# Loads of the cached values of sample batches 4 to 7 issued from ScalarE's queue instead of SyncE's, in a streaming encoder step

## The chip, the cores and the metric

The kernel runs on one core of one Trainium2 chip. The metric is the device time of one execution in microseconds (us). Before the change its median is 1579.01 us over 3 runs (1578.56 to 1579.61).

## What is computed

Two layers (`DEPTH` = 2) of a hybrid encoder run over 512 prompt tokens and 8 sample batches of 16 new tokens each. A layer has a combined input projection, three head groups side by side (retention, forgetting attention, a short convolution), an output projection and a gated feed-forward block. The part around the change is the forgetting attention of the sample batches: each batch's 16 new queries look at 512 cached keys and values and at their own 16 new ones.

```
def _fox_sample(q, k, v, logf, ck, cv, clogf):
    k_all = jnp.concatenate([ck.astype(k.dtype), k], axis=1)
    v_all = jnp.concatenate([cv.astype(v.dtype), v], axis=1)
    c_t = jnp.transpose(jnp.cumsum(lf_all, axis=1), (0, 2, 1))
    sc = jnp.einsum('bqhd,bkhd->bhqk', q, k_all, preferred_element_type=jnp.float32) * scale
    sc = sc + cq[..., None] - c_t[:, :, None, :]
    sc = jnp.where(mask, sc, -jnp.inf)
    p = jax.nn.softmax(sc, axis=-1)
    return jnp.einsum('bhqk,bkhd->bqhd', p.astype(v_all.dtype), v_all)
```

For each batch the cached keys are 512 x 512 float32 (1 MiB), and so are the cached values. The forget bias of a batch (`c_t` above, 8 heads x 512) is spread over 128 partitions by a third load of 256 KiB.

## The kernel before, in words

The program is written by hand for five engines, which meet through semaphores. Large matrix products run on TensorE (PE) as three products of rounded high and low parts, all of them recorded at line 2218; turns of tiles are at line 2280. The weights come in slabs of 512 KiB through `raw`, a buffer of three slots; ScalarE (ACT) rounds a slab into `whi` (`upto`, line 1145), VectorE (DVE) forms the rest `wlo` (line 1521).

Sample attention handles the batches n = 0 to 7 in a fixed pipeline:

- PE: `scores(n)` (line 2533) multiplies the queries of batch n with its cached keys; `turned(n)` turns the probabilities of batch n-1; `values(n)` multiplies them with the cached values of batch n-1. The order is `scores(1)`, then for n = 1 to 7 `turned(n)`, `scores(n + 1)`, `values(n)`; between the last steps the first products of the output projection are put (`out_slab`).
- DVE: `maxima(n)` (line 1954) adds the bias to the scores and takes the maximum; it waits for the bias load of the batch.
- ACT: `exps(n)` (line 1364) takes the exponential, and line 1241 copies the turned probabilities from the PSUM bank to `pTs`. After the copies of n = 5, 6 and 7 ACT rounds a weight slab.
- SyncE (SP) issues all loads, in the order in which its program has them, and where it waits for a semaphore everything behind that stands still.

The cached keys have five buffers and the cached values four, so a load waits until an earlier batch has used its buffer:

```
        kcache = (kb, kx, kbo, ky, kT)
        vcache = (vb[:, 0], vx[:, :, :], vb[:, 1], vr[:, :, :])
K_HOME = (0, 1, 2, 3, 4, 0, 2, 4)
V_HOME = (0, 1, 2, 3, 0, 2, 3, 0)
```

In what follows K4 to K7 are the key loads of batches 4 to 7 (`load_k`, line 749, into `kT`, `kb`, `kbo`, `kT`), V4 to V7 the value loads (`load_v`, line 753, into `vb`, `vb`, `vr`, `vb`) and P4 to P7 the bias loads (`load_pb`, line 850, into `pb`). `("ss", n)` is the bank of `scores(n)`, `("so", n)` the bank of the values product of batch n, and `smax` counts finished `maxima`. SP's order before is K4, K5, P4, V4, P5, K6, P6, V5, P7, K7, V6, V7, and then the weight slabs 31 to 33 (line 718), each of which waits until its slot is free.

Of the kernel before, what the change touches and what calls it, by code (L numbers as in the profile page):

```python
# [37 lines left out]
P = 128  # L38
D = 1024
KT = D // P  # L40
SEQ, NB, NS, PAST = 512, 8, 16, 512
# [211 lines left out]
V_HOME = (0, 1, 2, 3, 0, 2, 3, 0)  # L253
# [114 lines left out]
def build(nc, a):  # L368
    with ExitStack() as ctx:
        sems = {}  # L370

        def sem(name):
            sems[name] = ctx.enter_context(nc.semaphore(name))
            return sems[name]

        bank = [ctx.enter_context(nc.psum_tensor(f"bank{i}", [P, 512], F32)) for i in range(8)]
        B = Banks([sem(f"full{i}") for i in range(8)], [sem(f"free{i}") for i in range(8)])
# [32 lines left out]
        def K(name):  # L410
# [21 lines left out]
        fbias = own("fbias", [P, FH])  # L432
        ftap = own("ftap", [P, 2, 3])
        (fqg, fkg, gng, t2f, qbd, ncp, _, pb1, pb2) = region(
            [("fqg", [P, FW], F32), ("fkg", [P, FW], F32), ("gng", [P, RW], F32)],
            [("t2f", [P, 4, HALF], F32)],
            [("qbd", [P, 2, P], F32), ("ncp", [P, SEQ], F32)],
            [("by_qbd", [P, 2, P], F32), ("pb1", [P, PAST], F32), ("pb2", [P, PAST], F32)])
        (gains, os_, ncc, _, pb0) = region(
            [("gains", [P, D], F32)],  # L440
            [("os", [P, 4, P], F32), ("ncc", [P, PAST], F32)],
# [6 lines left out]
             ("t2h", [P, 4, HALF], F32R), ("t2l", [P, 4, HALF], F32R), ("s1", [P, 512], F32), ("s2", [P, 512], F32)])  # L448
        (gs, t4h) = region([("gs", [P, TT, RW], F32)], [("t4h", [P, 4, HALF], F32R)])
        (rT, kw, rv, decp, decq, st, _, decs, s0, _, lfxh, lfxl, kb, kT, vb, _, pTf, _, ycv, gpad, gu, _, lrows, t4l, s3, s4, _, _, _, h21, h22,  # L450
         _, _, _, xlo, xhi, _, pb3) = region(
            [("rT", [P, 4, NTOK], F32), ("kw", [P, TT, RW], F32), ("rv", [P, TT, RW], F32),
# [33 lines left out]
        vcache = (vb[:, 0], vx[:, :, :], vb[:, 1], vr[:, :, :])  # L486
# [57 lines left out]
        v_in = [sem(f"v_in{i}") for i in range(4)]  # L544
# [158 lines left out]
        def _(sp):  # L703
# [44 lines left out]
            def load_k(l, b):  # L748
                sp.dma_start(kcache[K_HOME[b]][:, :, :], kview[bass.ds(l * NB + b, 1)].rearrange("o p g n -> p (o g) n"))\
                    .then_inc(k_in[K_HOME[b]], 16)  # L750

            def load_v(l, b):
                sp.dma_start(vcache[V_HOME[b]], vview[bass.ds(l * NB + b, 1)].rearrange("o p k n -> p (o k) n"))\
                    .then_inc(v_in[V_HOME[b]], 16)
# [15 lines left out]
            for l in range(DEPTH):  # L770
# [113 lines left out]
                def next_pb(b):  # L884
                    sp.wait_ge(smax, l * NB + b - 3)
                    load_pb(b)
# [5 lines left out]
                B.wait_full(sp, ("ss", 0), l)  # L892
                load_k(l, 5)
                next_pb(4)
                B.wait_full(sp, ("so", 0), l)
                load_v(l, 4)
                next_pb(5)
                B.wait_full(sp, ("ss", 2), l)
                load_k(l, 6)
                next_pb(6)  # L900
                B.wait_full(sp, ("so", 2), l)
                load_v(l, 5)
                next_pb(7)
                B.wait_full(sp, ("ss", 4), l)
                load_k(l, 7)
                B.wait_full(sp, ("so", 3), l)
                load_v(l, 6)
                B.wait_full(sp, ("so", 4), l)
                load_v(l, 7)

                for n in range(31, 34):
                    load(n, l, slab_src(n, l))
# [224 lines left out]
        def _(act):  # L1137
# [9 lines left out]
            def upto(n, l):  # L1147

                while split_to[0] <= n:
                    if split_to[0] >= SLOTS or l == 0:  # L1150
                        wait_used(act, split_to[0] - SLOTS, l)
                    elif split_to[0] == 0:
                        B.wait_full(act, ("u", "loop", "a4"), l - 1, PAIRS - 2)
                    else:
                        B.wait_full(act, ("d", "end", split_to[0] - 1, TT - 1), l - 1)
                    split(split_to[0], l)
                    split_to[0] += 1
# [76 lines left out]
            for l in range(DEPTH):  # L1234
                split_to[0] = 0

                def evac(key, out, l, it=None, view=None):

                    B.wait_full(act, key, l, it)
                    src = bank[B.bank(key)][:, :] if view is None else view(bank[B.bank(key)])  # L1240
                    act.activation(out, src, ACT.Copy).then_inc(B.free[B.bank(key)], 1)
# [117 lines left out]
                def exps(n):  # L1359

                    act.wait_ge(smax, l * NB + n + 1)
                    o = SB + 8 * (n % 3)
                    for c0, n_, acc in ((0, PAST, 3), (PAST + NS * n, NS, 4)):
                        act.activation(ps[:, n % 2, c0:c0 + n_], ps[:, n % 2, c0:c0 + n_], ACT.Exp, scale=-1.0,
                                       bias=col(o + 2), accum_out=col(o + acc)).then_inc(sexp, 1)
# [2 lines left out]
                    exps(n)  # L1368
                for n in range(1, NB + 1):
                    evac(("pt", n - 1), pTs[:, (n - 1) % 2, 0:512], l)  # L1370
                    if n in (5, 6, 7):
                        B.wait_full(act, ("so", 3), l)
                        upto(WO + n - 5, l)
                    if n + 1 < NB:
                        exps(n + 1)
# [1395 lines left out]
```

## Time and profile before

| | |
|---|---|
| median of 3 runs | 1579.01 us (1578.56 to 1579.61) |
| the profiled execution: its own time | 1580.97 us |
| the profiled execution: span of the core | 1579.2 us |
| mean granted TensorE clock | 0.993 of full speed |
| PE busy | 1544.2 us, 98% of the span |
| DVE busy | 1053.8 us, 67% |
| ACT busy | 667.0 us, 42% |
| GpSimd busy | 401.5 us, 25% |
| moved by DMA | 168.02 MB, mean 106 GB/s |

The span runs from the first to the last instruction. PE is busy nearly all the time, so a microsecond in which it stands still is a microsecond of the total. The loads and stores are all but a few issued by SP and run on one hardware queue of the 16 DMA engines (queue q1 of the profile: 166.95 of the 168.02 MB). Engine names with a q behind them (SPq, ACTq) are the issuing of transfers, which is not counted as busy. "To landing" is the time from the issue of a transfer until its semaphore has its full count.

### The profile page before, as it was taken

To read this page: it belongs to the slowest core of one execution; us is meant where nothing else is said; L and a number is where in the kernel's file an instruction comes from. 1 tells how busy PE (TensorE), PEld (TensorE's weight loads), DVE (VectorE), ACT (ScalarE), POOL (GpSimd) and SP (SyncE) were. 2 spreads that over 40 slices of the span, in tenths; PEclk is the share of its full clock that TensorE was granted. 3 is DMA by queue.
4 is the path that set the end of the run, shared out by engine and by line. 5 is a ranking of instruction groups with operands and counts; after the bars stand their busy time and mean duration, and the time that the engine had idled before them with its cause. 6 is when DMAs were issued, how large, how long until landed. Compare 5 with 4: busy or idle time off the path is not lost.

```text
span 1579.2 us, 28383 instructions
## 1 busy us (share of the span) xinstructions
PE 1544.2 (98%) x9892; PEld 1347.8 (85%) x9892; DVE 1053.8 (67%) x1815; ACT 667.0 (42%) x1246; POOL 401.5 (25%) x505
## 2 busy tenths in 40 slices
PE   8999999799999999999999999988999999999998
PEld 6878896589999999999888789856899999999997
DVE  4445447339988888888654552662599888788885
ACT  4223327226444444444433233462365444444442
POOL 1113100004433333333112140000144333333330
PEclk9999999899999999999999999998999999999999
DMA  7213446622322222222242225574223222222222
GB/s 231 81 56 85 143 159 253 200 81 67 94 80 81 90 85 89 83 90 68 79 108 67 72 82 183 181 243 149 81 72 114 82 80 80 80 80 80 82 77 73
DMA packets 119005, 168.02 MB, mean 106 GB/s; under 512 B 28217, under 2 KB 80349, under 8 KB 114798
## 3 DMA queue, kind: packets, MB, share of 16 engines
q1 hardware_dynamic: 118784, 166.95, 33.9%
q8 instruction: 47, 0.77, 0.2%
q14 instruction: 28, 0.23, 0.0%
q10 hardware_dynamic: 146, 0.07, 0.0%
HBM read 157.11 MB, written 9.89 MB: 106 GB/s over the span
## 4 chain that ended last, share of the span: by engine, by line
PE 90%; DVE 4%; DMA 3%; ACT 1%; issue 1%; DVEq 0%; POOL 0%; POOLq 0%; SPq 0%; ACTq 0%
PE bank L2218 87%; PE bank L2280 3%; DMA kT<-in_cache_fox_k 2%; DVE pf L1881 0%; DMA raw<-in_w_gate 0%; DVE pf L1894 0%; DVE gulo L1545 0%; DMA raw<-in_w_in 0%; DVE x L2005 0%; DVE xn L1573 0%; DVE wlo L1535 0%; DVE wlo L1541 0%; POOLq L1112 0%; DVE wlo L1521 0%; POOL s L1110 0%
## 5 line engine op out<-in xcount | busy, mean ns | idle before, releaser
L2218 PE MATMUL bank<-whi,hhi 128*128 128x512 f32 x560 | 225.2, 402 | 0.9 <-DVE hlo L1545 0.6
L2218 PE MATMUL bank<-whi,hlo 128*128 128x512 f32 x560 | 219.4, 392 | 0.0
L2218 PE MATMUL bank<-wlo,hhi 128*128 128x512 f32 x560 | 218.9, 391 | 0.0
L2218 PE MATMUL bank<-hhi,whi 128*128 128x320 f32 x640 | 198.7, 310 | 0.8 <-DVE hlo L1545 0.8
L2218 PE MATMUL bank<-hhi,wlo 128*128 128x320 f32 x640 | 197.8, 309 | 0.0
L2218 PE MATMUL bank<-hlo,whi 128*128 128x320 f32 x640 | 197.6, 309 | 0.0
L2218 PE MATMUL bank<-whi,guhi 128*128 128x512 f32 x440 | 171.7, 390 | 0.4 <-DVE gulo L1545 0.4
L2218 PE MATMUL bank<-wlo,guhi 128*128 128x512 f32 x440 | 171.3, 389 | 0.0
L2218 PE MATMUL bank<-whi,gulo 128*128 128x512 f32 x440 | 171.2, 389 | 0.0
L1521 DVE TENSOR_TENSOR wlo<-raw,whi 128x1024 fp32r<-128x1024 f32 x80 | 100.1, 1251 | 106.5 <-ACT whi L1145 105.1
L2005 DVE TENSOR_TENSOR x<-x,bank 128x512 f32<-128x512 f32 x220 | 142.9, 682 | 29.0 <-PE bank L2218 27.5
L1145 ACT ACTIVATE whi<-raw 128x1024 fp32r<-128x1024 f32 x80 | 84.5, 1058 | 109.2 <-PE bank L2218 100.5
L2218 PEld LDWEIGHTS bank<-whi,hhi 128*128 128x128 f32 x560 | 105.7, 189 | 25.4 <-issue 3.0
L2218 PEld LDWEIGHTS bank<-whi,hlo 128*128 128x128 f32 x560 | 105.5, 188 | 22.9
L2218 PEld LDWEIGHTS bank<-wlo,hhi 128*128 128x128 f32 x560 | 105.9, 189 | 20.0
L2218 PEld LDWEIGHTS bank<-hhi,whi 128*128 128x128 f32 x640 | 120.2, 188 | 2.7 <-issue 1.9
L2218 PEld LDWEIGHTS bank<-hlo,whi 128*128 128x128 f32 x640 | 120.2, 188 | 0.8
L2218 PEld LDWEIGHTS bank<-hhi,wlo 128*128 128x128 f32 x640 | 120.1, 188 | 0.0
L1110 POOL TENSOR_TENSOR s<-raw 128x512 f32<-128x512 f32 x60 | 91.4, 1523 | 84.3 <-DMA raw<-in_w_gate 84.3
L1110 POOL TENSOR_TENSOR s<-raw,gains 128x512 f32<-128x512 f32 x20 | 27.3, 1363 | 311.0 <-DMA raw<-in_w_up 311.0
L990 POOL TENSOR_SCALAR small<-small 128x1 f32<-128x1 f32 (+2 forms) x42 | 12.3, 292 | 338.6 <-ACT xn L1218 214.8
L2218 PEld LDWEIGHTS bank<-whi,gulo 128*128 128x128 f32 x440 | 82.6, 188 | 17.4
(303 smaller groups left out, 3581.4 us busy)
## 6 DMA issues: line engine op xcount, KB each, us to landing
raw<-in_w_in SPq DMA_DIRECT2D x52, 512.0 KB, 3.7
raw<-in_w_gate SPq DMA_DIRECT2D x44, 512.0 KB, 3.8
raw<-in_w_down SPq DMA_DIRECT2D x44, 512.0 KB, 3.5
raw<-in_w_up SPq DMA_DIRECT2D x24, 512.0 KB, 3.7
vb<-in_cache_fox_v SPq DMA_DIRECT2D x10, 1024.0 KB, 9.6
gains<-in_w_up SPq DMA_DIRECT2D x20, 512.0 KB, 3.7
raw<-in_w_out SPq DMA_DIRECT2D x16, 512.0 KB, 3.8
bcr<-scr_p SPq DMA_DIRECT2D x8, 512.0 KB, 5.1
```

What stands on the lines that cost most here:

```text
L990: pool.tensor_scalar(col(var, n), col(ss, n), scale, EPS, ALU.mult, ALU.add)
L1110: pool.tensor_tensor(by_k(out[:, :]), x_, y_, op).then_inc(s_sum, 1)
L1145: act.activation(whi[:, slot(n), 0:width(n)], raw[:, slot(n), 0:width(n)], ACT.Copy).then_inc(hi_split, 1)
L1521: dve.tensor_tensor(wlo[:, s_, 0:w_], raw[:, s_, 0:w_], whi[:, s_, 0:w_].bitcast(F32), ALU.subtract).then_inc(lo_split, 1)
L2005: dve.tensor_tensor(x[:, t, 512 * c:512 * c + 512], x[:, t, 512 * c:512 * c + 512], bank[B.bank(key)][:, :], ALU.add).then_inc(B.free[B.ba ...
L2218: return pe.matmul(out, lhsT=lhsT, rhs=rhs, start=start, stop=stop, skip_group_check=True)
L2280: ins = pe.transpose(dst, src, ident[0:src.shape[0], 0:src.shape[0]])
```

## The change

SP no longer issues V4 to V7. Its waits for the banks `("so", 0)`, `("so", 2)`, `("so", 3)` and `("so", 4)` go with them. ACT issues the four loads instead, behind its copies of n = 2, 4, 5 and 6, with the same waits, the same addresses and the same buffers. The queue is then ACT's own. Nothing else is changed; V0 to V3 stay with SP.

```
                 load_k(l, 5)
                 next_pb(4)
-                B.wait_full(sp, ("so", 0), l)
-                load_v(l, 4)
                 next_pb(5)
                 B.wait_full(sp, ("ss", 2), l)
                 load_k(l, 6)
                 next_pb(6)
-                B.wait_full(sp, ("so", 2), l)
-                load_v(l, 5)
                 next_pb(7)
                 B.wait_full(sp, ("ss", 4), l)
                 load_k(l, 7)
-                B.wait_full(sp, ("so", 3), l)
-                load_v(l, 6)
-                B.wait_full(sp, ("so", 4), l)
-                load_v(l, 7)
...
                 for n in range(1, NB + 1):
                     evac(("pt", n - 1), pTs[:, (n - 1) % 2, 0:512], l)
+                    if n in (2, 4, 5, 6):
+                        b, before = {2: (4, 0), 4: (5, 2), 5: (6, 3), 6: (7, 4)}[n]
+                        B.wait_full(act, ("so", before), l)
+                        act.dma_start(vcache[V_HOME[b]], a["cache_fox_v"].rearrange("l b (p k) h d -> (l b) p k (h d)", p=P)
+                                      [bass.ds(l * NB + b, 1)].rearrange("o p k n -> p (o k) n")).then_inc(v_in[V_HOME[b]], 16)
                     if n in (5, 6, 7):
                         B.wait_full(act, ("so", 3), l)
                         upto(WO + n - 5, l)
```

On SP, from K5 to the weight slabs, the order before is the following (`full2` is the semaphore of a bank filled by `scores`, `full5` of the bank filled by `values`; buffer numbers stand behind `pb`):

```order
L749 DMA kb<-in_cache_fox_k 128x2048 [waits full2]
L850 DMA pb_87<-scr_c 128x1x512 [waits smax]
L753 DMA vb<-in_cache_fox_v 128x2048 [waits full5]
L850 DMA pb_81<-scr_c 128x1x512 [waits smax]
L749 DMA kbo<-in_cache_fox_k 128x2048 [waits full2]
L850 DMA pb_82<-scr_c 128x1x512 [waits smax]
L753 DMA vb<-in_cache_fox_v 128x2048 [waits full5]
L850 DMA pb_140<-scr_c 128x1x512 [waits smax]
L749 DMA kT<-in_cache_fox_k 128x2048 [waits full2]
L753 DMA vr<-in_cache_fox_v 128x2048 [waits full5]
L753 DMA vb<-in_cache_fox_v 128x2048 [waits full5]
L718 DMA raw<-in_w_out 128x2x512 [waits lo_split] x3
```

With the change it is this:

```order
L749 DMA kb<-in_cache_fox_k 128x2048 [waits full2]
L850 DMA pb_87<-scr_c 128x1x512 [waits smax]
L850 DMA pb_81<-scr_c 128x1x512 [waits smax]
L749 DMA kbo<-in_cache_fox_k 128x2048 [waits full2]
L850 DMA pb_82<-scr_c 128x1x512 [waits smax]
L850 DMA pb_140<-scr_c 128x1x512 [waits smax]
L749 DMA kT<-in_cache_fox_k 128x2048 [waits full2]
L718 DMA raw<-in_w_out 128x2x512 [waits lo_split] x3
```

The two V loads that stood ahead of K7 and the two that stood behind it are gone; P5 follows P4, P7 follows P6, and K7 follows P7.

On ACT, around the steps n = 4 to 6 of the sample batches, the changed kernel has this order (its lines stand 8 above those of the kernel before, so 1233 is the copy to `pTs`, 1356 `exps`, 1137 the rounding of a slab):

```order
L1233 ACTIVATE pTs<-bank 128x512 [waits full6]
L1366 DMA vb<-in_cache_fox_v 128x2048 [waits full5]
L1356 ACTIVATE ps,small<-ps,small 128x512 [waits smax]
L1356 ACTIVATE ps,small<-ps,small 128x16
L1233 ACTIVATE pTs<-bank 128x512 [waits full1]
L1366 DMA vr<-in_cache_fox_v 128x2048 [waits full5]
L1137 ACTIVATE whi<-raw 128x1024 [waits raw_in1,full0,full5]
L1356 ACTIVATE ps,small<-ps,small 128x512 [waits smax]
L1356 ACTIVATE ps,small<-ps,small 128x16
L1233 ACTIVATE pTs<-bank 128x512 [waits full6]
L1366 DMA vb<-in_cache_fox_v 128x2048 [waits full5]
```

V5, V6 and V7 now stand between a copy and the next exponentials, V6 also ahead of the rounding of a slab; V4 stands in the same way behind the copy of n = 2.

## Rows read from the trace of the kernel before

**Rows 1.** Page, part 4: the chain that ended last, by line

```profile
PE bank L2218 87%; PE bank L2280 3%; DMA kT<-in_cache_fox_k 2%; DVE pf L1881 0%; DMA raw<-in_w_gate 0%; DVE pf L1894 0%; DVE gulo L1545 0%; DMA raw<-in_w_in 0%; DVE x L2005 0%; DVE xn L1573 0%; DVE wlo L1535 0%; DVE wlo L1541 0%; POOLq L1112 0%; DVE wlo L1521 0%; POOL s L1110 0%
```

**Rows 2.** The chain in order of time: start us, us, what

```profile
278.84 15.61 DMA kT<-in_cache_fox_k
...
1060.74 14.98 DMA kT<-in_cache_fox_k
```

**Rows 3.** Timeline of PE, layer 0: start us, us, line, form, count [idle before <-releaser]

```profile
285.33 1.93 PE L2218 MATMUL bank<-kbo,qbd 128*32 128x512 f32 x8 [0.42 <-DMA kbo<-in_cache_fox_k]
...
294.49 1.93 PE L2218 MATMUL bank<-kT,qbd 128*32 128x512 f32 x8 [4.26 <-DMA kT<-in_cache_fox_k]
296.20 1.93 PE L2218 MATMUL bank<-vb,pTs 128*32 128x128 f32 x32
```

**Rows 4.** Timeline of PE, layer 1

```profile
1075.76 1.94 PE L2218 MATMUL bank<-kT,qbd 128*32 128x512 f32 x8 [4.18 <-DMA kT<-in_cache_fox_k]
```

**Rows 5.** Timeline of SP's issues, layer 0: P5, K6, P6, V5, P7, K7, V6, V7, slab

```profile
271.50 0.60 SPq L850 DMA_DIRECT2D pb<-scr_c  x1
272.14 0.46 SPq L749 DMA_DIRECT2D kbo<-in_cache_fox_k  x1
272.64 0.60 SPq L850 DMA_DIRECT2D pb<-scr_c  x1
277.83 0.32 SPq L753 DMA_DIRECT2D vb<-in_cache_fox_v  x1
278.19 0.60 SPq L850 DMA_DIRECT2D pb<-scr_c  x1
278.84 0.46 SPq L749 DMA_DIRECT2D kT<-in_cache_fox_k  x1
281.52 0.33 SPq L753 DMA_DIRECT2D vr<-in_cache_fox_v  x1
289.18 0.33 SPq L753 DMA_DIRECT2D vb<-in_cache_fox_v  x1
290.77 0.38 SPq L718 DMA_DIRECT2D raw<-in_w_out  x1
```

**Rows 6.** By tile, one issue each: time to landing of K6, V5, K7, V6, V7

```profile
DMA to landing us min/median/max: 13.1/13.1/13.1
...
DMA to landing us min/median/max: 12.5/12.5/12.5
...
DMA to landing us min/median/max: 15.6/15.6/15.6
...
DMA to landing us min/median/max: 15.4/15.4/15.4
...
DMA to landing us min/median/max: 10.2/10.2/10.2
```

**Rows 7.** Stretches: us, busy time of each engine, PEclk, DMA share, GB/s

```profile
267.50:294.50 27.00, 18.88 (x324) 11.00 (x325) 13.15 (x69) 11.77 (x34) 1.91 (x9) 0.89 0.99 325
...
278.00:280.50 2.50, 2.16 (x35) 0.91 (x37) 1.09 (x6) 1.43 (x5) 0.18 (x1) 1.00 1.00 231
...
292.00:295.50 3.50, 1.01 (x8) 0.35 (x12) 0.00 (x0) 0.00 (x0) 0.00 (x0) 0.51 0.95 374
```

**Rows 8.** By tile `vr`, whole run (V3 and V6 of both layers): time to landing

```profile
DMA to landing us min/median/max: 4.7/9.9/15.4
```

**Rows 9.** Timeline of ACT, layer 0, copies and exponentials of n = 4 to 6

```profile
278.86 0.57 ACT L1241 ACTIVATE pTs<-bank 128x512 f32<-128x512 f32 x1
...
284.18 0.58 ACT L1241 ACTIVATE pTs<-bank 128x512 f32<-128x512 f32 x1
...
288.52 0.72 ACT L1364 ACTIVATE ps<-ps,small 128x512 f32<-128x512 f32 x1 [2.82 <-DVE small L1958]
...
289.73 0.60 ACT L1241 ACTIVATE pTs<-bank 128x512 f32<-128x512 f32 x1
```

**Rows 10.** Timeline of DVE, layer 0, `maxima` of batch 6

```profile
287.44 0.69 DVE L1954 CUSTOM_DVE_ANT_0 ps<-bank,pb 128x512 f32<-128x512 f32 x1 [2.01 <-DMA pb<-scr_c]
```

More of the change, by code:

```diff
@@ L894, in _ @@
                 next_pb(4)
-                B.wait_full(sp, ("so", 0), l)
-                load_v(l, 4)
                 next_pb(5)
@@ L900, in _ @@
                 next_pb(6)
-                B.wait_full(sp, ("so", 2), l)
-                load_v(l, 5)
                 next_pb(7)
@@ L905, in _ @@
                 load_k(l, 7)
[L906 to L909, printed above, removed]
                 for n in range(31, 34):
@@ L1370, in _ @@
                     evac(("pt", n - 1), pTs[:, (n - 1) % 2, 0:512], l)
+                    if n in (2, 4, 5, 6):
+                        b, before = {2: (4, 0), 4: (5, 2), 5: (6, 3), 6: (7, 4)}[n]
+                        B.wait_full(act, ("so", before), l)
+                        act.dma_start(vcache[V_HOME[b]], a["cache_fox_v"].rearrange("l b (p k) h d -> (l b) p k (h d)", p=P)
+                                      [bass.ds(l * NB + b, 1)].rearrange("o p k n -> p (o k) n")).then_inc(v_in[V_HOME[b]], 16)
                     if n in (5, 6, 7):
```

## The prediction

> **What bounds the kernel now.** I read the chain of waits first. It is PE from end to end, and the only transfer in it with a share worth naming is the load of `kT` with 2% [rows 1]. In order of time that is one piece per layer, 15.61 and 14.98 us from issue to landing [rows 2]; it is K7, the keys of batch 7. So the place is the sample attention, and every microsecond by which K7 lands earlier or later moves all that comes after it.
>
> The timeline of PE says what K7 costs: PE stands still for 4.26 us before `scores(7)` in layer 0 and 4.18 us in layer 1 [rows 3, 4]. PE reached that point at 294.49 - 4.26 = 290.2 us. It also waited 0.42 us for K6 [rows 3], and DVE waited 2.01 us for P6 [rows 10]. All three waits are for loads of one family.
>
> The issues of SP [rows 5] and the times to landing [rows 6] then give the queue. K6 lands at 272.1 + 13.1 = 285.2, V5 at 277.8 + 12.5 = 290.3, K7 at 278.8 + 15.6 = 294.4, V6 at 281.5 + 15.4 = 296.9, V7 at 289.2 + 10.2 = 299.4. The loads land in the order of issue, and 1 MiB that took 4.7 us in a nearly empty queue [rows 8] takes 10 to 16 here. The stretches say why: from 267.5 to 294.5 the DMA engines are busy for a share of 0.99 [rows 7]. **The bound of this piece is the work in the DMA engines, not the moment at which SP issues.** Two prices follow from the differences of the landings. V6 and V7 cost 2.5 us each with nothing between them, P7 and K7 together 294.4 - 290.3 = 4.1. And of 4.7 us in an empty queue some 2.2 are not transfer (4.7 - 2.5), so a load begins to move about 2 us after its issue.
>
> **The change part by part.** A move on SP: K7 waits for `scores(4)` and stands behind V5 and P7. Without the V loads it is issued some 2 us sooner, since V5 at 277.83 and P7 are what stands right ahead of it [rows 5]. Worth: nothing, because K7 lies 15.6 us in a queue that is never empty; an earlier place in line only helps past what is ahead of it. The same goes for P5 and P6, K5 and K6. Their order among themselves stays.
>
> Four issues on ACT. An issue by SP takes 0.32 us [rows 5], and I take 0.4. The waits added before them are for values products that PE does before the turns whose result ACT has just copied, so they are met on arrival. Behind the issue stand the exponentials, and ACT stood still 2.82 us before those of batch 6 [rows 9], which hides the 0.4 us also where a slab is rounded between. Worth: nothing. If that cover went, it would be 4 x 0.4 = 1.6 us per layer.
>
> The new order in the DMA engines is what counts. Before, everything is served in one line: V4 and V5 ahead of K7, V6 and V7 behind it. Now the V loads have a line of their own. V4 and V5 are still served before K7 ends: V5 is issued behind the copy at 278.86 + 0.57 [rows 9], begins to move near 282 and has until 294. They cost K7 what they cost before. V6 is new ahead of K7. It is issued behind the copy that ends at 284.18 + 0.58 = 284.8 [rows 9], and moves from about 287. At 287 the SP line still holds part of P6, P7 and K7, and K7's landing is 7.4 us of work away, with V6 9.9. V6 needs 2.5 us of these 9.9, so it is done before K7 whenever ACT's line gets more than a quarter of the service. Cost: **+2.5 us per layer**.
>
> V7 is issued behind the copy at 289.73 + 0.60 [rows 9]. That copy stands behind the exponentials of batch 6, which need P6, and P6 is now late itself: in the one line it did not wait for V5, now V5 (2.5 us) and a part of V6 go between, some 3.5 us. So V7 is issued near 290.3 + 3.5 = 293.8 and moves from about 296, when K7 (due at 296.9) lacks about 1 us. It takes as much again from K7 if the two take turns. Cost: **+1.0 us per layer**.
>
> PE arrives at `scores(7)` later too, as K6 shares with V5 from 282 and lands up to 285.2 - 282 = 3.2 us, with turns half of it, later. PE is there near 292, still well before 297.9, so this adds nothing; the wait for K7 grows from 4.3 to near 6. Behind `scores(7)` the values of batches 5 and 6 find V5 and V6 landed, and V7 is wanted only after the first slabs of the output projection. The slab at 290.77 waits for its slot and not for SP [rows 5]. TensorE's granted clock is already at its lower level, 0.51 of full speed, which is 1.2 of 2.4 GHz, while PE waits for K7 [rows 7]; I add nothing for a longer wait.
>
> Sum: 2.5 + 1.0 = 3.5 us per layer, 7.0 us for two. The profiled execution has 1580.97 us (span 1579.2) and would come to 1588.0; it stands 1.96 above the median, so against the median the forecast is 1579.0 + 7.0 = **1586.0 us**.
>
> No row of this trace shows two lines that share the DMA engines. The bounds for that are these. At worst V6 and V7 both go whole before K7: 5.0 us per layer. At best SP's line is served first: K7 lands at least 2.5 us sooner and PE has it at about 291.9, but the next product needs V5, which then lands when K7 did, at 294.4, and that product began at 296.20 [rows 3]: -1.8 us per layer. I take a value near the upper end, because a quarter of the service for ACT's line is enough for the larger term.
>
> The Trainium skill, DMA: Bandwidth & Descriptors, section Queues, rings and completion order, has it that each DMA engine takes turns between the queues that have work, a packet at a time. By that rule V6 is served ahead of K7 and the sum is the +2.5 to +5.0 us per layer; without it -1.8 would be as good a guess. Its section Issuing engines are not separate DMA queues says that issuing from several engines saves only issue time, which speaks against the change. No run here shows either yet.
>
> **The rivals.** *The two lines together move more.* The rate while bias loads are under way falls to 231 GB/s, and without them it is 374; the mean over the piece is 325 [rows 7]. If packets of the other line filled these holes, the 27 us would become 27 x 325 / 374 = 23.5, that is 3.5 us less, just what the order costs: 1579 us, no change. Against it: the DMA share is 1.00 in the hole as well, so the engines were not idle in it. Half of that effect gives 1582.5.
>
> *SP's line is served first* (the other side). ACT's loads only get what is left. K7 then comes at once when its buffer and P7 allow, the wait of 4.26 us shrinks to what V5 needs, and the piece gains 1.8 us per layer: 1579.0 - 3.6 = 1575.4. It decides from the point where ACT's line gets under a quarter of the service after 287 us. For it: SP's loads are issued some 2 us earlier and stand in line in time. Against it: nothing in the rows favours a queue.
>
> *Nothing moves*, because K7 is not held up by what is ahead of it but by its own late issue. Then 2 us sooner would be 2 us gained per layer, 1575. Against it stand the landings in the order of issue.
>
> **How the numbers follow.** About 0.2%, 3.2 us, is what a measurement of this kernel tells from no change. The main case (V6, and V7 in part or whole, ahead of K7; 1584 to 1589) has 0.60, all slower. More throughput has 0.23: 0.17 of it within 0.2%, 0.03 just slower, 0.03 beyond it to faster. SP first or the late issue have 0.14: 0.11 faster, 0.03 within. The last 0.03 go to small mixed outcomes within 0.2%. That makes faster 0.14, within 0.23, slower 0.63. The range takes in the upper bound (1579 + 10 = 1589, and 1 us for a longer spell at the low clock) and the case of full throughput with some spread, 1577: 1577 to 1590.
>
> **What would show it.** In the changed profile queue q10 carries 8 MiB more. V6 lands before K7, K7 lands near 298 in layer 0 (294.4 before), PE waits near 6 us before `kT`, and DVE waits longer for P6 than 2.01 us. The forecast is wrong if V6 lands behind K7, if the rate of the piece is well over 325 GB/s, or if PE's wait for `kT` is shorter than 4.26 us.

## The result and the profile after

The changed kernel has a median of 1583.00 us over 9 runs (1578.09 to 1585.53), the kernel before 1579.01 us over 9 runs (1576.82 to 1580.57). The ratio is 1.0022, with a 95% interval from 1.0013 to 1.0031. By this ratio the change is 3.5 us slower (2.1 to 4.9); 7.0 us were forecast. The sign is right, the size is half. The profiled execution took 1582.30 us, its span is 1580.4 us.

The page of the changed kernel shows the eight loads on ACT's own queue, 8.46 MB on q10 in place of 0.07. The chain by line is as before [rows 1], with the load of `kT` at 2%.

```profile
span 1580.4 us, 28383 instructions
...
q1 hardware_dynamic: 117632, 158.56, 32.4%
q10 hardware_dynamic: 1298, 8.46, 1.5%
...
PE bank L2215 86%; PE bank L2277 3%; DMA kT<-in_cache_fox_k 2%; DVE pf L1878 0%; DMA raw<-in_w_gate 0%; DVE pf L1891 0%; DVE gulo L1542 0%; DVE x L2002 0%; DVE xn L1570 0%; DVE wlo L1532 0%; DVE wlo L1538 0%; ACT xn L1210 0%; DMA x<-in_x_prompt 0%; POOLq L1104 0%; DVE wlo L1518 0%
```

The issues of K4 and K7 by SP, and those of V5, V6 and V7 by ACT, in layer 0 of the changed kernel. SP issues K4 here at 264.83, 0.98 us earlier than before, by what happened long ahead of this place. So in what follows I count from the issue of K4.

```profile
264.83 0.33 SPq L749 DMA_DIRECT2D kT<-in_cache_fox_k  x1
...
275.65 0.33 SPq L749 DMA_DIRECT2D kT<-in_cache_fox_k  x1
```

```profile
277.41 0.33 ACTq L1366 DMA_DIRECT2D vb<-in_cache_fox_v  x1
...
281.52 0.33 ACTq L1366 DMA_DIRECT2D vr<-in_cache_fox_v  x1
...
291.61 0.72 ACT L1356 ACTIVATE ps<-ps,small 128x512 f32<-128x512 f32 x1 [8.29 <-DVE small L1955]
291.62 0.34 ACTq L1366 DMA_DIRECT2D vb<-in_cache_fox_v  x1
```

K7 is issued 10.8 us behind K4 (13.0 before, where K4 went out at 265.81), as SP no longer waits for values products. It lands 18.5 us after its issue, where it took 15.6 [rows 6]. V6 goes out at 281.52 and lands after 9.1 us, at 290.6, ahead of K7 (294.2); it landed behind it before. The times to landing, by tile, of K7, V6 and V7 of layer 0:

```profile
DMA to landing us min/median/max: 18.5/18.5/18.5
...
DMA to landing us min/median/max: 9.1/9.1/9.1
...
DMA to landing us min/median/max: 5.3/5.3/5.3
```

V7 is issued only at 291.62, in the same moment as the exponentials of batch 6, which had waited 8.29 us. What held them up is in the timelines of DVE and PE:

```profile
290.53 0.69 DVE L1951 CUSTOM_DVE_ANT_0 ps<-bank,pb 128x512 f32<-128x512 f32 x1 [7.48 <-DMA pb<-scr_c]
...
1072.93 0.69 DVE L1951 CUSTOM_DVE_ANT_0 ps<-bank,pb 128x512 f32<-128x512 f32 x1 [8.03 <-DMA pb<-scr_c]
```

```profile
284.06 1.94 PE L2215 MATMUL bank<-kbo,qbd 128*32 128x512 f32 x8 [1.52 <-DMA kbo<-in_cache_fox_k]
...
292.41 0.45 PE L2277 MATMUL bank<-const,ps 128*128 128x128 f32 x1 [4.04 <-issue]
...
294.24 1.94 PE L2215 MATMUL bank<-kT,qbd 128*32 128x512 f32 x8 [0.93 <-DMA kT<-in_cache_fox_k]
...
1077.03 1.94 PE L2215 MATMUL bank<-kT,qbd 128*32 128x512 f32 x8 [1.31 <-DMA kT<-in_cache_fox_k]
```

DVE waits 7.48 us for P6, against 2.01 [rows 10]. In DVE's program the scaling of batch 4's result stands behind `maxima(6)`, and PE's turn of that result, which stands ahead of `scores(7)`, waits for it. So the stop shows up on PE as 4.04 us at line 2277, and the wait at `kT` is short, 0.93 and 1.31 us, against 4.26 and 4.18 [rows 3, 4]. Reading only the wait that had been named before, one would call the change a gain. Counted from K4's issue, `scores(7)` begins at 29.4 and 30.3 us in the two layers, and began at 28.7 and 28.4: 0.7 and 1.9 us later.

Two stretches of layer 0 show a thing I had not read before (the last two columns are the DMA share and GB/s):

```profile
278.00:280.50 2.50, 2.38 (x53) 1.36 (x56) 1.41 (x8) 0.85 (x4) 0.46 (x2) 1.00 1.04 433
...
288.00:292.00 4.00, 0.38 (x4) 0.14 (x2) 1.23 (x8) 0.39 (x1) 0.00 (x0) 0.84 0.51 202
```

From 288 to 292, while P6 and K7 are still missing, the DMA engines are busy for a share of 0.51 only, and move 202 GB/s; from 278 to 280.5 it was 433. The share is a mean over 16 engines. I read it as half of them having nothing to do and the rest being late; e4 puts this to the test.

### The profile page after: what moved, and what is told of

The parts are those of the page before. It is cut to its first block, busy times and chain, and to the rows that moved or that the text cites. A ratio compares the mean times of both kernels' runs of the same rounds, so it can differ in the third digit from the quotient of the medians.

```text
span 1580.4 us, 28383 instructions
## 1 busy us (share of the span) xinstructions
PE 1544.4 (98%) x9892; PEld 1347.4 (85%) x9892; DVE 1053.5 (67%) x1815; ACT 666.3 (42%) x1246; POOL 401.4 (25%) x505
## 3 DMA queue, kind: packets, MB, share of 16 engines
q10 hardware_dynamic: 1298, 8.46, 1.5%
## 4 chain that ended last, share of the span: by engine, by line
PE 90%; DVE 4%; DMA 3%; ACT 1%; issue 1%; POOL 0%; DVEq 0%; POOLq 0%; SPq 0%; ACTq 0%
PE bank L2215 86%; PE bank L2277 3%; DMA kT<-in_cache_fox_k 2%; DVE pf L1878 0%; DMA raw<-in_w_gate 0%; DVE pf L1891 0%; DVE gulo L1542 0%; DVE x L2002 0%; DVE xn L1570 0%; DVE wlo L1532 0%; DVE wlo L1538 0%; ACT xn L1210 0%; DMA x<-in_x_prompt 0%; POOLq L1104 0%; DVE wlo L1518 0%
## 5 line engine op out<-in xcount | busy, mean ns | idle before, releaser
L2002 DVE TENSOR_TENSOR x<-x,bank 128x512 f32<-128x512 f32 x220 | 142.8, 681 | 29.2 <-PE bank L2215 28.5
```

The costliest lines, as they stand in the source:

```text
L2002: dve.tensor_tensor(x[:, t, 512 * c:512 * c + 512], x[:, t, 512 * c:512 * c + 512], bank[B.bank(key)][:, :], ALU.add).then_inc(B.free[B.ba ...
```

## The experiments

"K7 at" is the start of `scores(7)` in layer 0 and layer 1, counted from K4's issue, from the one profiled execution of each kernel. Each kernel was timed against the kernel before on the same chip (medians of before: 1579.75, 1580.05 and 1579.88 us in the three sets).

| run | edit | median us | ratio (95%) | K7 at |
|---|---|---|---|---|
| before | | 1579.01 | | 28.7, 28.4 |
| the change | V4 to V7 on ACT | 1583.00 | 1.0022 (1.0013 to 1.0031) | 29.4, 30.3 |
| e1 | V4, V5 on ACT | 1579.91 | 1.0002 (0.9993 to 1.0011) | 28.1, 28.8 |
| e2 | V6, V7 on ACT | 1589.04 | 1.0054 (1.0040 to 1.0067) | 33.3, 33.6 |
| e3 | the change, V6 and V7 one step later | 1577.28 | 0.9984 (0.9975 to 0.9993) | 29.1, 27.4 |
| e4 | before, bias source of 16 rows | 1572.49 | 0.9950 (0.9937 to 0.9964) | 24.7, 25.2 |
| e5 | the change, bias source of 16 rows | 1574.90 | 0.9965 (0.9951 to 0.9978) | 23.6, 28.5 |
| e6 | before, V5 issued behind K7 | 1577.05 | 0.9983 (0.9974 to 0.9992) | 26.3, 26.7 |
| e7 | e1 with e4 | 1571.59 | 0.9942 (0.9929 to 0.9956) | 23.4, 25.0 |
| e8 | e6 with e4 | 1568.73 | 0.9926 (0.9912 to 0.9939) | 23.7, 23.8 |
| e9 | before, V6 and V7 held until K7 has landed | 1578.02 | 0.9989 (0.9980 to 0.9998) | 27.5, 27.7 |
| e10 | before, V7 held until K7 has landed | 1578.82 | 0.9998 (0.9989 to 1.0007) | 28.9, 28.0 |

In layer 0 of six of these profiles (e3, e4, e5, e7, e8, e10) PE also stops inside a values product for 1.8 to 3.8 us, with no releaser that the profile names; in layer 1 only e8 has such a stop (2.0 us). In before, the change, e1, e6 and e9 there is none over 0.6 us. So in layer 0 of those six "K7 at" can hide a wait for K7 or be late by itself, and I give K7's landing where it matters.

**e1 and e2: which half of the change costs.** In e1 only V4 and V5 are left on ACT, in e2 only V6 and V7.

```
e1 (against the change)
                 load_k(l, 7)
+                B.wait_full(sp, ("so", 3), l)
+                load_v(l, 6)
+                B.wait_full(sp, ("so", 4), l)
+                load_v(l, 7)
-                    if n in (2, 4, 5, 6):
+                    if n in (2, 4):
e2 (against the change)
                 next_pb(4)
+                B.wait_full(sp, ("so", 0), l)
+                load_v(l, 4)
...
                 next_pb(6)
+                B.wait_full(sp, ("so", 2), l)
+                load_v(l, 5)
-                    if n in (2, 4, 5, 6):
+                    if n in (5, 6):
```

> Half of the change is taken back: V4 and V5 stay on ACT, V6 and V7 are issued by SP behind K7 as before. Theory (order): the loss comes from V6 being served ahead of P6 and K7, so it goes: 1578 to 1580 us, K7 lands within 1 us of where it lands before, and DVE's wait for P6, 7.5 us in the changed kernel, falls under 4. Rival (two lines as such cost, through turns between queues or through ACT's issues): two of four moved loads keep at least half of the loss, 1581 us or more.

> The other half alone: V4 and V5 are issued by SP as before, V6 and V7 by ACT. Theory (order): the whole loss is here, 1582 to 1584 us, V6 lands before K7, DVE waits 6 us or more for P6 or PE over 5 us for K7. Rival (two lines as such cost): about half of the loss, 1581 us.

The time of e1 is that of the kernel before, and `scores(7)` begins within 0.6 us of where it did. So the second line as such costs nothing that can be measured, and neither do the two issues left on ACT. One expectation of e1 missed: DVE still waits 5.51 and 6.93 us for P6, not under 4. V5, issued by ACT, still lies beside P6. The wait for P6 only splits PE's wait otherwise; where K7 lands decides.

e2 takes 1589.04 us, where I expected 1582 to 1584: it is slower than the change itself. The timeline of PE in e2:

```profile
298.67 1.93 PE L2219 MATMUL bank<-kT,qbd 128*32 128x512 f32 x8 [8.74 <-DMA kT<-in_cache_fox_k]
...
1084.90 1.93 PE L2219 MATMUL bank<-kT,qbd 128*32 128x512 f32 x8 [9.69 <-DMA kT<-in_cache_fox_k]
```

Here P6 is on time (DVE waits 2.22 us for it), so V7 is issued 24.0 and 23.4 us behind K4 instead of 26.8 and 27.3. V6 lands well ahead of K7, and V7 within 0.5 us of it (299.0 against 298.6 in layer 0), so V7 is served beside K7. K7 comes 4.6 and 5.2 us later than before. Two whole value loads at 2.5 us each are 5.0: the upper bound of the prediction, measured. In the change V7 goes out 3 to 4 us later, because the late P6 holds back the step behind which ACT issues it. Of the two moves the one of V6 and V7 is the harmful one, and the one of V4 and V5 softened it.

**e3: V6 behind the step that needs P6.**

```
-                    if n in (2, 4, 5, 6):
-                        b, before = {2: (4, 0), 4: (5, 2), 5: (6, 3), 6: (7, 4)}[n]
+                    if n in (2, 4, 6, 7):
+                        b, before = {2: (4, 0), 4: (5, 2), 6: (6, 3), 7: (7, 4)}[n]
```

> All four on ACT, but V6 is issued behind the copy of n = 6 and V7 behind that of n = 7. Theory (order): V6 can no longer be ahead of P6, since the step n = 6 needs P6 done; DVE's wait for P6 falls under 5 us and most of the loss goes, 1579 to 1581 us. Rival (two lines as such cost): 1582 to 1584 us as in the changed kernel. If V6 now comes too late for its own product, PE waits for vr and the time is above 1584.

It is 0.16% faster than the kernel before and so beats my expectation. V6 now goes out 28.1 and 24.7 us behind K4, where it went at 16.7 and 17.2. DVE's wait for P6 in layer 1 is 5.4 us, slightly over the 5 I gave. Layer 0 of this profile can't be used for P6, as PE stopped there inside a values product, and the rest had time to catch up (at 1579.08 us the profiled execution is also one of the slowest of this kernel):

```profile
281.57 0.31 PE L2215 MATMUL bank<-vb,pTs 128*32 128x128 f32 x3 [3.77 <-issue]
```

In layer 1 K7 comes at 27.4 against 30.3 in the change and 28.8 in e1. All four loads are still on ACT's queue, so this separates the order from the queue once more: ACT's queue costs nothing as long as V6 and V7 stay out of K7's way.

**e4: the bias loads on all 16 DMA engines.** A bias load reads 8 rows (one for each head) and repeats each 16 times. In e4 each row stands twice in the scratch tensor, and the load reads 16 rows with 8 repeats. A load still brings 256 KiB.

```
-        scr_c = nc.dram_tensor("scr_c", [DEPTH, NB * FH, PAST], F32).ap()
+        scr_c = nc.dram_tensor("scr_c", [DEPTH, NB * FH, 2, PAST], F32).ap()
-                sp.dma_start(scr_c[l], ncc[0:NB * FH, :]).then_inc(nc_out, 16)
+                sp.dma_start(scr_c[l], ncc[0:NB * FH, :].unsqueeze(1).to_broadcast([NB * FH, 2, PAST])).then_inc(nc_out, 16)
-                                 bass.AP(scr_c.tensor, (l * NB + b) * FH * PAST, [[PAST, FH], [0, NS], [1, PAST]]))\
+                                 bass.AP(scr_c.tensor, (l * NB + b) * FH * 2 * PAST, [[PAST, 2 * FH], [0, NS // 2], [1, PAST]]))\
```

> The kernel before, with each row of the bias scratch in DRAM written twice, so that the source of a bias load has 16 rows with 8 repeats instead of 8 rows with 16 repeats. Theory (half of the DMA engines carry the bias loads: share 0.49 to 0.55 where only late work is left): the bias loads spread over all 16, P4 to P7 cost half, K7 lands 3 to 5 us sooner, PE's wait of 4.3 us shrinks under 1, and the time is 1569 to 1574 us. Rival (the holes in the rate come from the repeated reads of few bytes): nothing changes, 1578 to 1580 us, and the share falls to about 0.5 behind K7 as before.

0.50% faster, 7.9 us by the ratio. K7 lands 24.2 us behind K4's issue in layer 0, 4.4 us sooner than before, though it was issued 1.6 us later. There `scores(7)` no longer waits, but partly because PE had stopped for 2.87 us just ahead of it. In layer 1 `scores(7)` begins 3.2 us earlier and still waits 4.13 us, as PE comes to it sooner too; the wait was to shrink under 1 us, so that part missed. The stretch from 267.5 to 294.5 moves 351 GB/s, against 325 [rows 7]:

```profile
267.50:294.50 27.00, 20.58 (x377) 11.70 (x375) 15.52 (x78) 13.58 (x38) 1.87 (x8) 1.00 0.98 351
```

```profile
288.79 0.43 PE L2218 MATMUL bank<-vb,pTs 128*32 128x128 f32 x8 [2.87 <-issue]
...
290.38 1.04 PE L2218 MATMUL bank<-kT,qbd 128*32 128x512 f32 x8
...
1067.21 1.94 PE L2218 MATMUL bank<-kT,qbd 128*32 128x512 f32 x8 [4.13 <-DMA kT<-in_cache_fox_k]
```

This, with the share of 0.51 while late loads are left over, is what a placement of the bias loads on half of the engines predicts. The Trainium skill, DMA: Bandwidth & Descriptors, section Why a DMA increments its semaphore by 16 and not by 1, has the rule: the number of DMA engines is the largest up to 16 that divides the slowest dimension of both sides, here 8. The traces agree: the share is 0.51 in the changed kernel, 1.02 in its place with 16 rows (e5, below), and the edit gives 7.9 us back. The repeats also fall from 16 to 8, and no run separates the two: they may have had a part in the 7.9 us.

**e5: the change on top of e4.** The edit is that of e4 in the changed kernel.

> The changed kernel with the bias scratch doubled as in e4. Theory (the loss is order, and its size is the backlog of the eight DMA engines that carry the bias loads): P6 lands at least 3 us sooner than in the changed kernel, DVE's wait for it falls from 7.5 us under 3, and the time is 1572 to 1577 us, 0 to 4 us above e4 (1572.5). Rival (V6 ahead of K7 costs its 2.5 us per layer whatever the bias loads do): 1577 us or more, 5 us above e4.

DVE does not wait for P6 in layer 0 and waits 2.30 us in layer 1, and `maxima(6)` begins 6 us sooner than in the changed kernel. The time stands 2.4 us above e4, inside what the theory gave. e7 has the same bias loads and V6, V7 on SP, and is 3.3 us faster than e5. So V6 and V7 on ACT still cost as much in all when the bias loads are cheap (3.1 us between the change and e1), but all of it now lies in layer 1: `scores(7)` begins at 28.5 there against 25.0 in e7, and in layer 0 at 23.6 against 23.4. In layer 0 V6 lands behind K7 (290.8 against 287.7), so it was not ahead of it. In layer 1 PE waits 5.91 us for K7.

Layer 0 of e5 is also the fair comparison for the share of 0.51. The loads are issued in the order of the changed kernel, V7 again only at 288.06, and up to K7's landing at 287.7 all DMA engines are busy:

```profile
284.00:287.70 3.70, 1.93 (x47) 1.34 (x44) 1.39 (x8) 1.27 (x5) 0.00 (x0) 1.00 1.02 414
```

**e6: one line, other order.**

```
                 next_pb(6)
-                B.wait_full(sp, ("so", 2), l)
-                load_v(l, 5)
                 next_pb(7)
                 B.wait_full(sp, ("ss", 4), l)
                 load_k(l, 7)
+                B.wait_full(sp, ("so", 2), l)
+                load_v(l, 5)
```

> One line as before, but SP issues V5 behind K7 instead of ahead of P7 and K7. Theory (order alone decides): K7 lands about 2.5 us sooner, PE's wait for K7 falls from 4.3 to about 2 us, then the product of batch 5 waits for V5, which lands near where K7 landed; net gain 1 to 2 us per layer, 1575 to 1577 us. Rival (order does not matter, only the sum of work up to V5): 1578 to 1580 us.

```profile
291.86 1.93 PE L2218 MATMUL bank<-kT,qbd 128*32 128x512 f32 x8 [1.55 <-DMA kT<-in_cache_fox_k]
...
1073.95 1.93 PE L2218 MATMUL bank<-kT,qbd 128*32 128x512 f32 x8 [2.41 <-DMA kT<-in_cache_fox_k]
```

K7 comes 2.4 and 1.8 us sooner, PE's wait for it falls to 1.55 and 2.41 us, and the time by 0.17%. V5 is now the load that comes last (PE's weight load waits 2.3 us for it in layer 0), as the "SP first" rival of the prediction had it.

**e7 and e8: the two orders with e4.** The edits are those of e1 and e6 together with e4's.

> V4 and V5 on ACT, V6 and V7 on SP behind K7 (e1), with the doubled bias scratch. Theory: with V6 behind K7, and P6 and K7 cheap, SP's earlier issue of K7 is worth something at last: K7 waits under 2 us in both layers (4.1 in layer 1 of e4), 1568 to 1572 us, below e4. Rival (two lines give nothing beside one): 1572 to 1573 us as e4.

> One line, K7 issued ahead of V5 (e6), with the doubled bias scratch. Theory: K7 is in time in both layers and V5 too, 1567 to 1571 us, below e4 (1572.5) by the 4.1 us wait of its layer 1. Rival (V5 becomes the wait in K7's place): 1572 us.

e7 has 1571.59 and e4 1572.49 us, with intervals that overlap; whether the second line gives anything there is open. K7 is waited for 2.53 us in its layer 1, more than expected. e8 is the fastest kernel of the study, 1568.73 us, 0.74% under the kernel before and some 15 us under the change by the two ratios. Neither layer waits for K7 any more, though each has a stop of 2.0 us without a releaser ahead of `scores(7)`, which would cover a short wait:

```profile
289.59 1.92 PE L2218 MATMUL bank<-kT,qbd 128*32 128x512 f32 x8
...
1064.91 1.04 PE L2218 MATMUL bank<-kT,qbd 128*32 128x512 f32 x8
```

**e9 and e10: why V6 cost less than its 2.5 us.** Between e1 and the change only V6 and V7 move, and K7 comes 1.3 and 1.5 us later for the two together, less than the 2.5 of V6 alone. The idea: when half of the DMA engines have run out of work, the late half is faster. To test it I kept the one line of before and held back what the leading half could run ahead into.

```
e9
                 load_k(l, 7)
+                wait_cached(sp, k_in, K_HOME, 7, l)
                 B.wait_full(sp, ("so", 3), l)
                 load_v(l, 6)
e10
                 load_v(l, 6)
+                wait_cached(sp, k_in, K_HOME, 7, l)
                 B.wait_full(sp, ("so", 4), l)
                 load_v(l, 7)
```

> The kernel before with one more wait on SP: V6, and V7 behind it, are issued only when K7 has landed. In one line neither is ahead of K7, so by order alone K7 lands where it lands before (28.7 and 28.4 us behind K4's issue) and the time is 1579 to 1580 us. Theory (the eight DMA engines without bias loads run ahead into V6 and V7 and slow the eight that are behind): with nothing to run ahead into they fall idle, and K7 lands 1 to 2 us sooner, 1576 to 1578 us. Rival (the halves do not disturb each other): K7 within 0.3 us of before; V6 then lands near 5 us behind K7, just in time, and a miss there would make the time longer.

> The same with V7 alone held until K7 has landed; V6 is issued as before. This is how late V7 comes in the changed kernel. Theory (halves disturb each other): K7 lands some 0.5 to 1 us sooner than before, 1578 to 1579 us. Rival: nothing changes.

In e9 K7 comes 1.2 and 0.7 us sooner, although nothing ahead of it was changed; the time falls by 0.11%, with an interval that stays under 1. A stretch of e9, where as I read it late loads alone move:

```profile
286.00:288.00 2.00, 2.00 (x44) 1.92 (x36) 1.19 (x7) 0.48 (x1) 0.00 (x0) 0.50 0.55 204
```

204 GB/s at a share of 0.55 are 23 GB/s for each busy DMA engine (204 / (16 x 0.55)), and it is 202 at 0.54 in the next 2 us. In the kernel before, from 288 to 290, all are busy with 288 GB/s:

```profile
288.00:290.00 2.00, 2.00 (x37) 1.42 (x30) 1.44 (x9) 1.38 (x5) 0.00 (x0) 0.83 1.06 288
```

That is 17 GB/s for each (288 / (16 x 1.06)), a mean over both halves. That K7 comes about 1 us sooner when V6 and V7 are held back is measured; that the late half runs faster because the other is idle is my reading of it. Busy neighbours alone don't slow an engine down: from 278 to 280.5 the changed kernel moved 433 GB/s at a share of 1.04, 26 for each.

e10 is in the range of the theory by its time alone (1578.82 us), but its interval includes 1. K7 comes 0.5 us sooner in layer 1; layer 0, 0.2 us later, is no test, since K7 was issued there 15.0 us behind K4 instead of 13.0 after a stop of PE. V7 alone has little effect on K7 in the old order. And e2 speaks against the idea as the full account: its DMA engines also ended half idle, and K7 came later by nearly the whole 5.0 us all the same:

```profile
296.00:298.50 2.50, 0.00 (x0) 0.00 (x0) 0.00 (x0) 0.00 (x0) 0.00 (x0) 0.50 0.45 181
```

## Why the prediction was right or wrong

*The bound* was right: the DMA engines' work ahead of K7, and not SP's issue. K7 went out 2.2 us sooner (10.8 against 13.0) and landed later; in e1 it went out as early and nothing was gained. So the third rival, a gain by the earlier issue, is out. e6 shows from the other side that the order in line is worth time: 0.17% for one swap.

*Four issues on ACT at nothing* was right. e1 has two of them and the time of before, e3 has all four and is faster; the rows show an issue taking 0.33 to 0.34 us beside ACT's own work.

*V4 and V5 at nothing* was right: e1, K7 at -0.6 and +0.4 us.

*V6 at +2.5 and V7 at +1.0 us per layer* is the step that failed: the terms are of the right kind and the wrong size. V6 was served ahead of K7 as said, and V7 beside the last of it, as the DMA share is back at 1.00 from 292.5 to 295. But the two together put K7 back by 1.3 and 1.5 us (the change against e1), or 0.7 and 1.9 (against before), where the sum had 3.5. V6's term alone was too large, since both came to less than it. How the 1.3 and 1.5 split between V6 and V7 is open, as no run has V6 alone on ACT.

I had priced a load at 2.5 us from the differences of landings in a stretch where all DMA engines are busy, and added it to a backlog. In the change the share falls to about half for some 4 us ahead of K7, so by my reading the backlog is of half of the DMA engines only. With V6 gone early and V7 not yet there the other half falls idle, and the late half speeds up. e9 measures what holding V6 and V7 back is worth: 1.2 and 0.7 us. That is near what is missing, but e2 pays nearly its full 5.0 us with a half-idle end as well. Why V6 and V7 cost less than half of their price in the change was not shown.

Nor were the two terms independent, as the sum had them: V7 is issued behind a step that needs P6. On K4's clock P6 was 4.1 us late in layer 0 (25.7 against 21.6) and 5.0 in layer 1 (26.2 against 21.2), where I had 3.5. In e2, where P6 is in time, V7 goes out 3 to 4 us earlier, and V6 and V7 cost 4.6 and 5.2. V7 was issued 26.8 us behind K4, near the 28.0 I had, and K7 landed 2.5 us after that, at 29.3 in place of some 32.

*PE's wait for K7 near 6 us* was wrong, it is 0.93 and 1.31. I followed PE only through its own loads, and left out that the turn before `scores(7)` needs a DVE instruction that stands behind the wait for P6. The cost is paid at line 2277. This was one of my signs that the forecast would be wrong (a wait shorter than 4.26 us), and it says nothing of the order, which e1 to e3 bear out. The error did not change the sum, because K7 lands behind P6 anyway, and so e1 could keep a wait of 5.5 to 6.9 us for P6 and lose no time.

*The rate.* The first rival had the lines together moving more, with 3.5 us to gain. In its stated form it is not borne out: from 267.5 to 294.5 the change moved 313 GB/s, less than 325. The 433 GB/s from 278 to 280.5, against 231 before [rows 7], are no gain of this kind: the hole only lies earlier in the change (228 GB/s from 272.5 to 275).

Over the two layers `scores(7)` comes 2.6 us later than before and 2.8 later than in e1, and 3.5 us (2.1 to 4.9) were measured. The direction was forecast for the right reason; the size of the two terms was not.

## What to carry to other kernels

When a stage is bound by work in the DMA engines, as here, a second issuing queue changes the order of service and not the amount of work. Ask of each load that it moves what it is now ahead of, and keep loads with slack behind the one that is waited for. Here one such swap within one queue (e6, 0.17%) was worth as much as the second queue with the order put right (e3, 0.16%). Look at the DMA share while something is being waited for: a share near 0.5 can mean that only half of the engines have the late work, and the shape of a small load can be the cause (e4, 0.50%).

## What the runs showed of the hardware that was not expected

- With bias loads whose source has 8 rows outermost, the DMA share fell to 0.51 at 202 GB/s for 4 us while loads were late (the change). With 16 rows and the same order it stayed at 1.02 with 414 GB/s up to K7 (e5, layer 0), and the kernel before gained 7.9 us for 0.26 MB more traffic (e4).
- While about half of the DMA engines were busy they moved some 23 GB/s each (e9), and while all were busy from 17 (before, 288 to 290) to 26 (the change, 278 to 280.5). Whether the bias reads or the mixture with 8 KiB rows is the cause was not tried.
- A load on ACT's queue went out at 281.52 while ACT's copy ahead of it in the program started at 281.80: in these rows the issue is not held back by the arithmetic ahead of it. V7 went out at 291.62, when the semaphore of the exponentials was there, and the copy ahead of it started at 292.62. V6 went out 16.7 us behind K4 where I had counted on 19.0. About 0.9 of that comes from not waiting for the copy's start and end (0.3 and 0.6), the other 1.4 from the copy itself, which came sooner because P5 did.
